# A product of 128 x 256 moved from GpSimd to VectorE in the gated stage of an expert layer

## The chip, the cores and the metric

The kernel runs on one core of one Trainium2 chip. The metric is the device time of one execution in microseconds (us). Engines are written as in the profile: PE is TensorE, DVE is VectorE, ACT is ScalarE, POOL is GpSimd, SP is the queue that issues most DMAs.

## The reference, cut to what matters

The whole kernel computes two transformer blocks on 256 tokens of width 1024. The change lies in the last layer, a mixture of 16384 experts of which each token takes 128 (8 heads of 16), each weighted by a gate:

```python
xb = tokens                                   # (t, 1024)
u = jnp.take(u_tab, eb, axis=0)               # experts' input rows
a = jax.nn.gelu(jnp.einsum('td,thkd->thk', xb, u), approximate=False)
w = (gb * a)                                  # gate x gelu
vv = jnp.take(v_tab, eb, axis=0)
y = jnp.einsum('thk,thkd->td', w, vv)
```

The kernel gathers nothing. It computes gelu(x u) for all 16384 experts, multiplies it by a dense matrix of gates that is zero for the experts not taken, and multiplies the result by the whole value table.

## The kernel before

**The weights' stream.** All weights come as one stream of 512 KB blocks through a ring of four slots. ScalarE copies a block to a rounded form (`w_high`, L496), VectorE subtracts that from the block (`w_low`, L1005, called split below), and TensorE makes each product as three matmuls: high x high, low x high, high x low (L1750 to L1752). A slot is loaded again once it is split.

**The expert layer.** The 16384 experts are 128 blocks of 128. `GE` (in the profile `expert_w`) holds for each block n and each of 256 tokens the product gate x gelu. For the first 66 blocks ScalarE writes the gelu straight into the block's slot. From then on gates are applied while the other blocks are still being computed: this is the gated stage, steps s = 2 to 63, block 64 + s. Slots not yet computed were filled with ones by GpSimd (L458 to L465). In each step

- TensorE computes block 64 + s (`u_block`, 24 matmuls of 256 columns) and then the dense gates of a group of four tokens, group s - 2 (`gates`, eight matmuls, L2311 and L2312), from one-hot tiles.
- ScalarE (`u_tile`) takes the gelu of block 64 + s into one half of a buffer (`GELU`, L921), makes the rounded copy of a later weight block (L496), and scales the one-hots of key 1 by the gates in four instructions (`gate_key1`, L931). `u_tile` waits until the product of block 62 + s has read its half of the buffer.
- GpSimd (`product`, L467 to L474) multiplies the gelu into the block's slot of `GE`.
- VectorE runs, in this order: `weigh` (L1679), which multiplies the gates of one group into four token columns of all 128 slots; `low1` (L1670), the low part of the gates on the one-hots; `hot2` (L1661), the one-hot of key 2 for the next group; a split (L1005); and `hot1` (L1653), the one-hot of key 1, in a single buffer that `gate_key1` and `low1` read.

**What sets the order.** Each engine's order is written out by hand. `weigh` touches all slots and a product touches one slot in all columns, so they must alternate: `product(s)` waits for `weighed` >= s - 2 and the next `weigh` waits for `prod_ok`. In VectorE's loop, step s = 4 i + q, weigh(s - 3) waits for the gates of group s - 3 and for `prod_ok` >= s - 2, which is the product of block 64 + s - 1. The loops on all engines are `Fori(1, 16)`: 15 turns of four steps, s = 4 to 63. Ahead of the loop stand the first product(s), the first weighing and the one-hots of groups 0 to 2; behind it the last groups, interleaved with the first four value blocks, whose weights are split into high and low from `GE` in halves (L968, L1713). Then comes the value stage, 128 blocks of 12 matmuls of 512 columns.

The order of VectorE's loop is this:

```python
with dve.Fori(1, STEPS // 4) as i:
    for q in range(4):
        weigh(q - 3, i * 4, 1)
        low1(q - 2, i * 4)
        hot2(q - 1, i * 4)
        split(b + STEP0 + 3 + q, 1, i * 4)
        hot1(q - 1, i * 4)
```

Of the kernel before, what the change touches and what calls it, by code (L numbers as in the profile page):

```python
# [13 lines left out]
ALU = mybir.AluOpType  # L14
# [42 lines left out]
EXPERT_BLOCKS = 128  # L57
# [5 lines left out]
STEP0 = 64  # L63
FIRST_GATED = STEP0 + 2
STEPS = EXPERT_BLOCKS - STEP0
# [33 lines left out]
def at(static, dyn=None, scale=1):  # L99

    return static if dyn is None else dyn * scale + static


def build(nc, stream, w_dt, cols, small_row, rows, x, mem, keys, out):
# [3 lines left out]
    def sb(name, shape, kb, dt=F32):  # L108
        return nc.alloc_sbuf_tensor_at(name, shape, dt, offset=B0 + int(kb * KB))

    def sem(name):
        return ctx.enter_context(nc.semaphore(name))
# [119 lines left out]
    GELU = sb("gelu_out", [P, 2, SEQ], 75.5)  # L232


    GE = sb("expert_w", [P, EXPERT_BLOCKS, SEQ], 79)
# [105 lines left out]
    tops_ok, gelu_ok, weighed, prod_ok = sem("tops_ok"), sem("gelu_done"), sem("group_weighed"), sem("block_weighed")  # L341
    slots_one, wt_high, wt_low = sem("slots_one"), sem("weighted_high"), sem("weighted_low")
# [36 lines left out]
    def _(pool):  # L379
# [84 lines left out]
        pool.wait_ge(hot_one, 4)  # L464
        pool.memset(GE[:, 80:105, :], 1.0).then_inc(slots_one, 1)  # L465

        def product(s, dyn=None, late=True):  # L467

            pool.wait_ge(gelu_ok, at(STEP0 + s + 1, dyn))
            if late:  # L470
                pool.wait_ge(weighed, at(s - 2, dyn))
            n = STEP0 + s
            slot = GE[:, n, :] if dyn is None else GE[:, bass.ds(dyn + n, 1), :].rearrange("p a t -> p (a t)")
            pool.tensor_tensor(slot, slot, GELU[:, s % 2, :], ALU.mult).then_inc(prod_ok, 1)  # L474

        pool.wait_ge(slots_one, 3)
        product(2, late=False)
        product(3)
        with pool.Fori(1, STEPS // 4) as i:
            for q in range(4):  # L480
                product(q, i * 4)
        pool.dma_start(LAST_GAIN[:], rows[4].partition_broadcast(P)).then_inc(row_in, 16)


# [513 lines left out]
    def _(dve):  # L998
        chain = Chain(dve, dve_chain)

        def split(n0, count, dyn=None):

            for n in range(n0, n0 + count):
                dve.wait_ge(w_high, at(n + 1, dyn))
                dve.tensor_tensor(WL[:, n % SLOTS, :], RING[:, n % SLOTS, :],  # L1005
                                  WH[:, n % SLOTS, :].bitcast(F32), ALU.subtract).then_inc(w_split, 1)
# [355 lines left out]
        for tt in range(TT):  # L1362
            dve.wait_ge(xs_sc, tt + 1)
            s = slice(tt * 4, tt * 4 + 4)
            chain(dve.reduce_max(STAT[:, 24:32][:, s], ACC[:, tt, :].rearrange("p (h m) -> p h m", h=4), AX_X))
            dve.tensor_scalar(STAT[:, 32:40][:, s], STAT[:, 24:32][:, s], -1.0 / 16, None, ALU.mult).then_inc(xs_max, 1)
        for tt in range(TT):
            dve.wait_ge(xs_exp, tt + 1)
            s = slice(tt * 4, tt * 4 + 4)
# [273 lines left out]
        def pairs(row, g, dyn):  # L1643

            t = bass.ds(at(GROUP * g, dyn, GROUP), GROUP)
            return row[:, t].rearrange("p (a b) -> p a b", b=2).unsqueeze(2).to_broadcast([P, GROUP // 2, P, 2])

        def hot1(g, dyn=None):

            if dyn is not None or g >= 1:  # L1650
                dve.wait_ge(key1_ok, at(g, dyn))
                dve.wait_ge(low1_ok, at(g, dyn))
            dve.tensor_tensor(OAE[:], IOTA16[:].unsqueeze(1).to_broadcast([P, GROUP // 2, P, 2]),  # L1653
                              pairs(KEY_T[:, 0, :], g, dyn), ALU.is_equal).then_inc(one1_ok, 1)

        def hot2(g, dyn=None):

            if dyn is not None or g >= 2:
                dve.wait_ge(g_ps, at(g - 1, dyn))
            t = bass.ds(at(GROUP * g, dyn, GROUP), GROUP)  # L1660
            dve.tensor_tensor(OB[:, g % 2, :, :], IOTA[:].unsqueeze(1).to_broadcast([P, GROUP, P]),  # L1661
                              KEY_T[:, 1, t].unsqueeze(2).to_broadcast([P, GROUP, P]),
                              ALU.is_equal).then_inc(key2_ok, 1)

        def low1(g, dyn=None):

            dve.wait_ge(one1_ok, at(g + 1, dyn))
            if dyn is not None or g >= 2:
                dve.wait_ge(g_ps, at(g - 1, dyn))
            dve.tensor_tensor(OAL[:, g % 2, :, :, :], OAE[:], pairs(GATE_LOW, g, dyn), ALU.mult).then_inc(low1_ok, 1)  # L1670

        def weigh(g, dyn=None, blocks=None):

            dve.wait_ge(g_ps, at(g + 1, dyn))
            if blocks:
                dve.wait_ge(prod_ok, at(g + blocks, dyn))
            w = GE[:, :, bass.ds(at(GROUP * g, dyn, GROUP), GROUP)]
            o = 1024 + g % 2 * 512
            dve.scalar_tensor_tensor(w, PS[:, o:o + 512].rearrange("p (t n) -> p n t", n=P), 1.0 / GATE_SCALE, w,  # L1679
                                     ALU.mult, ALU.mult).then_inc(weighed, 1)  # L1680

        split(b + STEP0 + 4, 2)
        dve.wait_ge(rt_ok, 2)
        dve.wait_ge(iota_ok, 2)
# [6 lines left out]
        low1(1)  # L1691
        dve.wait_ge(slots_one, 3)
        dve.wait_ge(gelu_ok, FIRST_GATED)
        dve.wait_ge(prod_ok, 1)
        weigh(0)
        hot2(2)
        hot1(2)
        with dve.Fori(1, STEPS // 4) as i:
            for q in range(4):
                weigh(q - 3, i * 4, 1)  # L1700
                low1(q - 2, i * 4)
                hot2(q - 1, i * 4)
                split(b + STEP0 + 3 + q, 1, i * 4)
                hot1(q - 1, i * 4)
        low1(STEPS - 2)
        split(m + 3, 1)
        hot2(STEPS - 1)
# [722 lines left out]
```

## Time and profile before

| | us |
|---|---|
| median of 3 runs | 1722.03 (1719.54 to 1722.96) |
| profiled execution, its own time | 1721.7 |
| its span in the trace | 1720.0 |
| TensorE busy | 1672.3 (97%) |
| VectorE busy | 1190.6 (69%) |
| ScalarE busy | 934.2 (54%) |
| GpSimd busy | 114.5 (7%) |
| gated stage, from the first product to the last | 1140.86 to 1360.59 |

The 1.7 us between span and time lie around the traced instructions. Shares over the whole span mix stages with different limits: the gated stage takes some 220 us of it. The ends of matmuls are modelled, so the distance between starts says more on TensorE than its busy time. A start in the timeline is when the engine began an instruction; the next one can start before the end shown.

### The profile page before, as it was taken

The numbers are of one execution on the slowest core, as the hardware profiler recorded it, in microseconds if no ns is written. First come the engines' busy times: TensorE is split into PE (matmuls) and PEld (weight loads), VectorE is DVE, ScalarE is ACT, GpSimd is POOL, SyncE is SP. The second block draws the span as 40 slices with busy tenths as digits, with TensorE's granted clock in tenths as the row PEclk, the third lists the DMA queues.
The fourth block names the chain that finished last, engine by engine and source line by source line (L and its number), as shares of the span: only waits on it lengthen the run. The fifth ranks groups of instructions, "written<-read, shape, count | busy, mean of one in ns | idle before, by whom it ended". The sixth has DMA issues, their size and how long they took to land.

```text
span 1720.0 us, 30593 instructions
## 1 busy us (share of the span) xinstructions
PE 1672.3 (97%) x10346; PEld 1482.4 (86%) x10346; DVE 1190.6 (69%) x1827; ACT 934.2 (54%) x1540; POOL 114.5 (7%) x106
## 2 busy tenths in 40 slices
PE   7999999989998999999989999999999999999998
PEld 6888898889897788879979999999999888888887
DVE  5555687487666555466664799989999866666664
ACT  5445546476655544456354444467777654455554
POOL 0000004000000000010010000112222200000000
PEclk9999999989999999999999999999999999999999
DMA  7555453323453555645344455444444365665663
GB/s 260 186 183 183 171 196 123 111 97 124 153 190 123 171 183 184 192 144 187 125 163 158 161 169 195 169 162 146 147 147 148 132 209 193 195 193 190 192 194 122
DMA packets 78814, 286.79 MB, mean 167 GB/s; under 512 B 8864, under 2 KB 9120, under 8 KB 78624
## 3 DMA queue, kind: packets, MB, share of 16 engines
q1 hardware_dynamic: 77888, 282.27, 49.4%
q0 software_dynamic: 864, 3.67, 0.6%
q8 instruction: 41, 0.67, 0.2%
q14 instruction: 21, 0.17, 0.0%
HBM read 284.86 MB, written 1.05 MB: 166 GB/s over the span
## 4 chain that ended last, share of the span: by engine, by line
PE 79%; DVE 10%; issue 6%; ACT 4%; DVEq 1%; DMA 0%; ACTq 0%; POOL 0%; SPq 0%; POOLq 0%
PE ps L1750 24%; PE ps L1752 24%; PE ps L1751 24%; DVE one_at_key L1653 3%; DVE w_low L1005 3%; ACT gate_high_at_key L931 1%; DVE gate_low_at_key L1670 1%; ACT w_high L496 1%; PE ps L1757 1%; PE ps L1839 1%; DVE xT_low L1039 0%; DVE tmp L1090 0%; ACT xn L512 0%; PE ps L2276 0%; DVE h L1092 0%
## 5 line engine op out<-in xcount | busy, mean ns | idle before, releaser
L1005 DVE TENSOR_TENSOR w_low<-ring,w_high 128x1024 fp32r<-128x1024 f32 x532 | 654.2, 1232 | 341.4 <-ACT w_high L496 339.3
L496 ACT ACTIVATE w_high<-ring 128x1024 fp32r<-128x1024 f32 x532 | 559.4, 1056 | 319.2 <-PE ps L1752 312.4
L1750 PE MATMUL ps<-xT_high,w_high 128*128 128x256 f32 x1600 | 462.1, 289 | 1.9 <-DVE xT_low L1039 1.9
L1751 PE MATMUL ps<-xT_high,w_low 128*128 128x256 f32 x1600 | 454.2, 284 | 0.0
L1752 PE MATMUL ps<-xT_low,w_high 128*128 128x256 f32 x1600 | 454.1, 284 | 0.0
L1750 PEld LDWEIGHTS ps<-xT_high,w_high 128*128 128x128 f32 x1600 | 308.2, 193 | 5.9 <-DVE w_low L1005 2.3
L1751 PEld LDWEIGHTS ps<-xT_high,w_low 128*128 128x128 f32 x1600 | 308.4, 193 | 0.7 <-issue 0.5
L1752 PEld LDWEIGHTS ps<-xT_low,w_high 128*128 128x128 f32 x1600 | 308.0, 193 | 0.0
L1750 PE MATMUL ps<-w_high,expert_w_high 128*128 128x512 f32 x512 | 200.5, 392 | 0.4 <-DVE expert_w_low L1713 0.4
L1751 PE MATMUL ps<-w_high,expert_w_low 128*128 128x512 f32 x512 | 200.0, 391 | 0.0
L1752 PE MATMUL ps<-w_low,expert_w_high 128*128 128x512 f32 x512 | 200.0, 391 | 0.0
L1750 PE MATMUL ps<-w_high,xT_high 128*128 128x512 f32 x464 | 187.1, 403 | 11.5 <-DVE xT_low L1039 6.4
L1752 PE MATMUL ps<-w_low,xT_high 128*128 128x512 f32 x464 | 183.4, 395 | 0.0
L1751 PE MATMUL ps<-w_high,xT_low 128*128 128x512 f32 x464 | 183.4, 395 | 0.0
L980 ACT ACTIVATE expert_w_high<-expert_w 128x256 fp32r x124 | 51.8, 418 | 164.9 <-PE ps L1752 164.9
L1750 PEld LDWEIGHTS ps<-w_high,xT_high 128*128 128x128 f32 x464 | 88.7, 191 | 31.5 <-DVE w_low L1005 7.6
L1750 PEld LDWEIGHTS ps<-w_high,expert_w_high 128*128 128x128 f32 x512 | 96.6, 189 | 20.7 <-issue 0.6
L1751 PEld LDWEIGHTS ps<-w_high,expert_w_low 128*128 128x128 f32 x512 | 96.6, 189 | 19.9
L1752 PEld LDWEIGHTS ps<-w_low,expert_w_high 128*128 128x128 f32 x512 | 96.5, 189 | 19.9
L931 ACT ACTIVATE gate_high_at_key<-one_at_key,gate_high 128x128 f16<-128x128 f16 x256 | 82.0, 391 | 52.5 <-DVE one_at_key L1653 52.5
L1731 DVE TENSOR_TENSOR expert_w_low<-expert_w,expert_w_high 128x256 fp32r<-128x256 f32 x124 | 52.7, 425 | 82.3 <-ACT expert_w_high L980 82.3
L1752 PEld LDWEIGHTS ps<-w_low,xT_high 128*128 128x128 f32 x464 | 88.6, 191 | 19.1
(373 smaller groups left out, 2115.1 us busy)
## 6 DMA issues: line engine op xcount, KB each, us to landing
ring<-in_stream SPq DMA_DIRECT2D x532, 512.0 KB, 3.4
row_gain<-in_rows POOLq DMA_DIRECT2D x4, 512.0 KB, 4.4
h<-in_x SPq DMA_DIRECT2D x2, 512.0 KB, 4.3
mem_sb<-in_mem SPq DMA_DIRECT2D x1, 1024.0 KB, 11.3
keys_sb<-in_keys POOLq DMA_DIRECT2D x1, 1024.0 KB, 5.3
out<-result SPq DMA_DIRECT2D x2, 512.0 KB, 2.6
last_gain<-in_rows POOLq DMA_DIRECT2D x1, 512.0 KB, 4.8
cols<-in_cols SPq DMA_DIRECT2D x1, 78.5 KB, 7.4
```

What stands on the lines that cost most here:

```text
L496: act.activation(WH[:, n % SLOTS, :], RING[:, n % SLOTS, :], ACT.Copy).then_inc(w_high, 1)
L931: last = act.activation(OAH[:, g % 2, j, :], OAE[:, j // 2, :, j % 2], ACT.Copy, scale=gate)
L980: act.activation(WTH[:, v % 4, :], slot, ACT.Copy).then_inc(wt_high, 1)
L1005: dve.tensor_tensor(WL[:, n % SLOTS, :], RING[:, n % SLOTS, :], WH[:, n % SLOTS, :].bitcast(F32), ALU.subtract).then_inc(w_split, 1)
L1653: dve.tensor_tensor(OAE[:], IOTA16[:].unsqueeze(1).to_broadcast([P, GROUP // 2, P, 2]), pairs(KEY_T[:, 0, :], g, dyn), ALU.is_equal).then_ ...
L1670: dve.tensor_tensor(OAL[:, g % 2, :, :, :], OAE[:], pairs(GATE_LOW, g, dyn), ALU.mult).then_inc(low1_ok, 1)
L1731: dve.tensor_tensor(WTL[:, v % 4, :], slot, WTH[:, v % 4, :].bitcast(F32), ALU.subtract).then_inc(wt_low, 1)
L1750: pe.matmul(out, high, w_hi, start=start, stop=False, skip_group_check=True)
L1751: pe.matmul(out, low, w_hi, start=False, stop=False, skip_group_check=True)
L1752: return pe.matmul(out, high, w_lo, start=False, stop=stop, skip_group_check=True)
L1757: last = pe.transpose(xt_psum(k, tt)[:, kt, :], XN[:, tt, kt * P:(kt + 1) * P], IDENT[:])
L1839: last = pe.transpose(hidden_psum(p)[:, o:o + P], HN[:, parity, tt, ft * P:(ft + 1) * P], IDENT[:])
```

## The change

GpSimd's product of each of the 62 blocks becomes an instruction of VectorE (`block_weighed`), with the same operands and the same waits. In step s of the loop it handles block 64 + s - 1 and stands first; `low1` moves ahead of `weigh`, so that it lies between the product and the weighing that waits for it. The first product stands ahead of the first weighing and the last one behind the loop. GpSimd keeps one wait for the last gelu, ahead of its load of the last gain. The buffers stay as they are.

```diff
@@ block.gpsimd
-        def product(s, dyn=None, late=True):
-
-            pool.wait_ge(gelu_ok, at(STEP0 + s + 1, dyn))
-            if late:
-                pool.wait_ge(weighed, at(s - 2, dyn))
-            n = STEP0 + s
-            slot = GE[:, n, :] if dyn is None else GE[:, bass.ds(dyn + n, 1), :].rearrange("p a t -> p (a t)")
-            pool.tensor_tensor(slot, slot, GELU[:, s % 2, :], ALU.mult).then_inc(prod_ok, 1)
-
-        pool.wait_ge(slots_one, 3)
-        product(2, late=False)
-        product(3)
-        with pool.Fori(1, STEPS // 4) as i:
-            for q in range(4):
-                product(q, i * 4)
+        pool.wait_ge(gelu_ok, EXPERT_BLOCKS)
         pool.dma_start(LAST_GAIN[:], rows[4].partition_broadcast(P)).then_inc(row_in, 16)
@@ block.vector
+        def block_weighed(s, dyn=None, late=True):
+
+
+            dve.wait_ge(gelu_ok, at(STEP0 + s + 1, dyn))
+            if late:
+                dve.wait_ge(weighed, at(s - 2, dyn))
+            n = STEP0 + s
+            slot = GE[:, n, :] if dyn is None else GE[:, bass.ds(dyn + n, 1), :].rearrange("p a t -> p (a t)")
+            dve.tensor_tensor(slot, slot, GELU[:, s % 2, :], ALU.mult).then_inc(prod_ok, 1)
+
@@
         dve.wait_ge(slots_one, 3)
         dve.wait_ge(gelu_ok, FIRST_GATED)
+        block_weighed(2, late=False)
         dve.wait_ge(prod_ok, 1)
         weigh(0)
         hot2(2)
         hot1(2)
         with dve.Fori(1, STEPS // 4) as i:
             for q in range(4):
+                block_weighed(q - 1, i * 4)
+                low1(q - 2, i * 4)
                 weigh(q - 3, i * 4, 1)
-                low1(q - 2, i * 4)
                 hot2(q - 1, i * 4)
                 split(b + STEP0 + 3 + q, 1, i * 4)
                 hot1(q - 1, i * 4)
+        block_weighed(STEPS - 1)
         low1(STEPS - 2)
         split(m + 3, 1)
         hot2(STEPS - 1)
```

## Rows read from the trace of the kernel before

**Rows 1.** page, part 1: busy time, share of span, instructions

```profile
PE 1672.3 (97%) x10346; PEld 1482.4 (86%) x10346; DVE 1190.6 (69%) x1827; ACT 934.2 (54%) x1540; POOL 114.5 (7%) x106
```

**Rows 2.** busy time by stretch, 13 turns; last columns: clock, DMA share, GB/s

```profile
1159.40:1345.10 185.70, 184.17 (x1666) 174.41 (x1665) 185.70 (x261) 135.87 (x313) 54.74 (x52) 1.00 0.44 147
```

**Rows 3.** timeline of TensorE, one turn; columns: start us, us, engine, line

```profile
1215.96 0.23 PE L2311 MATMUL ps<-gate_high_at_key,one_at_key 128*128 128x128 f16 x1
...
1216.53 0.38 PE L1750 MATMUL ps<-xT_high,w_high 128*128 128x256 f32 x1
...
1219.60 0.23 PE L2311 MATMUL ps<-gate_high_at_key,one_at_key 128*128 128x128 f16 x1
...
1230.82 0.38 PE L1750 MATMUL ps<-xT_high,w_high 128*128 128x256 f32 x1
```

**Rows 4.** timeline of TensorE, way in and first turn

```profile
1147.88 0.28 PE L1752 MATMUL ps<-xT_low,w_high 128*128 128x256 f32 x1
1148.00 0.23 PE L2311 MATMUL ps<-gate_high_at_key,one_at_key 128*128 128x128 f16 x1
...
1148.44 0.37 PE L1750 MATMUL ps<-xT_high,w_high 128*128 128x256 f32 x1
...
1151.39 0.23 PE L2311 MATMUL ps<-gate_high_at_key,one_at_key 128*128 128x128 f16 x1
```

**Rows 5.** timeline of ScalarE beside one steady step; brackets: idle before, releaser

```profile
1218.19 1.28 ACT L931 ACTIVATE gate_high_at_key<-one_at_key,gate_high 128x128 f16<-128x128 f16 x4 [0.80 <-DVE one_at_key L1653]
1219.70 0.38 ACT L921 ACTIVATE gelu_out<-ps 128x256 f32<-128x256 f32 x1 [0.23 <-PE ps L1752]
```

**Rows 6.** timeline of VectorE, one steady step

```profile
1217.09 0.96 DVE L1653 TENSOR_TENSOR one_at_key<-iota,keysT 128x512 f16<-128x512 f16 x1
1217.99 0.69 DVE L1679 SCALAR_TENSOR_TENSOR expert_w<-ps,expert_w 128x512 f32 x1
1218.60 0.41 DVE L1670 TENSOR_TENSOR gate_low_at_key<-one_at_key,gate_low 128x512 f16<-128x512 f16 x1
1218.93 0.69 DVE L1661 TENSOR_TENSOR one_at_key<-iota,keysT 128x512 f16<-128x512 f32 x1
1219.54 1.22 DVE L1005 TENSOR_TENSOR w_low<-ring,w_high 128x1024 fp32r<-128x1024 f32 x1
1220.67 0.97 DVE L1653 TENSOR_TENSOR one_at_key<-iota,keysT 128x512 f16<-128x512 f16 x1
```

**Rows 7.** timeline of VectorE, way in and first turn

```profile
1142.83 0.42 DVE L1653 TENSOR_TENSOR one_at_key<-iota,keysT 128x512 f16<-128x512 f16 x1
1143.17 0.68 DVE L1661 TENSOR_TENSOR one_at_key<-iota,keysT 128x512 f16<-128x512 f32 x1
...
1148.90 0.42 DVE L1653 TENSOR_TENSOR one_at_key<-iota,keysT 128x512 f16<-128x512 f16 x1
```

**Rows 8.** timeline of GpSimd, its products

```profile
1140.86 0.74 POOL L474 TENSOR_TENSOR expert_w<-expert_w,gelu_out 128x256 f32<-128x256 f32 x1 [20.94 <-ACT gelu_out L921]
...
1148.88 1.03 POOL L474 TENSOR_TENSOR expert_w<-expert_w,gelu_out 128x256 f32 x1 [2.90 <-ACT gelu_out L921]
...
1216.69 1.07 POOL L474 TENSOR_TENSOR expert_w<-expert_w,gelu_out 128x256 f32 x1 [2.49 <-ACT gelu_out L921]
1220.35 1.01 POOL L474 TENSOR_TENSOR expert_w<-expert_w,gelu_out 128x256 f32 x1 [2.58 <-ACT gelu_out L921]
```

**Rows 9.** timeline of VectorE, value stage: a 128x256 subtraction

```profile
1375.25 0.42 DVE L1731 TENSOR_TENSOR expert_w_low<-expert_w,expert_w_high 128x256 fp32r<-128x256 f32 x1
1375.59 1.23 DVE L1005 TENSOR_TENSOR w_low<-ring,w_high 128x1024 fp32r<-128x1024 f32 x1
```

**Rows 10.** timeline of TensorE, way out of the gated stage

```profile
1358.80 0.23 PE L2311 MATMUL ps<-gate_high_at_key,one_at_key 128*128 128x128 f16 x1
...
1363.42 0.77 PE L1750 MATMUL ps<-w_high,expert_w_high 128*128 128x512 f32 x1 [0.45 <-DVE expert_w_low L1713]
```

**Rows 11.** busy time by stretch, six microseconds at the way out

```profile
1362.00:1368.00 6.00, 5.21 (x25) 3.99 (x25) 3.85 (x11) 2.36 (x9) 0.00 (x0) 0.72 0.60 228
```

## The prediction

> **What bounds the kernel now.** I read the page first. TensorE is busy for 97% of the span [rows 1], so time comes off only where TensorE waits or is paced by another engine. The next view is the table of busy time by stretch, for the 13 turns of the loop in which all units of the gated stage run evenly. VectorE is busy for all of its 185.70 us [rows 2]. TensorE seems full there too (184.17), but its ends are modelled, so I go by its starts. One turn of four steps takes 14.29 us (1230.82 - 1216.53 in [rows 3]; 185.7 / 13 gives the same), or 3.57 a step. Where nothing held TensorE, in the first turn of the loop, a block's 24 matmuls took 2.95 from their first start to the first gate matmul (1148.44 to 1151.39) and the eight gate matmuls 0.44 (1148.00 to 1148.44) [rows 4]. Closing a turn costs 0.13 to 0.14 more (0.14 taken): 0.57 instead of 0.44 from the gates' first matmul to the next block (1215.96 to 1216.53) [rows 3]. So TensorE alone would need 4 x 3.39 + 0.14 = 13.70 a turn, 0.59 less than it takes. In the steady loop the gates start later than that, just behind ScalarE: its four gate copies end at 1218.19 + 1.28 = 1219.47 [rows 5] and the gates start at 1219.60 [rows 3]. The copies themselves had stood idle 0.80 for VectorE's one-hot [rows 5]. VectorE is the pace maker.
>
> **Where VectorE's 3.57 goes.** One step, start to start [rows 6]: hot1 (L1653) 0.90, weigh 0.61, low1 0.33, hot2 0.61, split 1.13. Sum 3.58. Only hot1 is odd. It takes 0.96 here, but 0.42 with a start-to-start of 0.34 at 1142.83, the same shape [rows 7]. What differs is GpSimd: its product starts at 1216.69, ahead of hot1 at 1217.09, and ends at 1217.76; hot1 ends at 1218.05, 0.29 later [rows 6, 8]. The next one ends at 1221.36 and its hot1 (started 1220.67, 0.97 long) at 1221.64, 0.28 later. So hot1 stands until the product is over and then does its own work. Order matters: at 1148.88 and 1148.90 the two started together, hot1 took its 0.42, and the product stretched to 1.03 against 0.74 for one beside an idle VectorE [rows 7, 8].
>
> **Part by part.** *Removed: 62 products on GpSimd.* Nothing of GpSimd's 0.7 to 1.1 us is on the path as work, but each product holds hot1 for 0.90 - 0.34 = 0.56 of VectorE's time. Gone: -0.56 a step. The POOL queue keeps one wait for the last gelu, as early as before to within the stage's own gain, and behind it the load of the last gain, which is needed only at the end of the kernel: 0. SP's queue gets nothing.
>
> *Added: 62 products on VectorE.* The nearest row is the subtraction over 128x256 float32 from two SBUF tiles, 0.42 long, with the next instruction 0.34 after its start (1375.25 to 1375.59) [rows 9]. I take 0.34; bounds 0.34 and 0.42. VectorE's step becomes 3.58 - 0.56 + 0.34 = 3.36, 13.44 a turn, which is under TensorE's 13.70.
>
> A rule says otherwise. The Trainium skill, VectorE: DVE Perf Modes, section "The DRAIN you can't avoid", holds that a next instruction does not start until the pipe of the one before is empty. By that the product would cost its whole 0.42 and the two short ones around it the same, 3.36 + 3 x 0.08 = 3.60, and nothing would be gained. The trace disagrees: starts 0.34 apart behind instructions of 0.42 [rows 7, 9].
>
> *Waits.* The product waits for ScalarE's gelu, which starts right behind the block's matmuls and lasts 0.38 [rows 5]; behind it in the queue stand low1, weigh, hot2, split and hot1. What TensorE needs of these first is low1, for gates a whole block of matmuls (2.95) later, and hot1, whose copies take 0.13 + 1.28 on ScalarE and are wanted one step after that. Both have slack once VectorE's step is under TensorE's, so the wait costs 0. The product also waits for the weighing two steps back (long done). ScalarE's gelu waits for the product that read the same half of the buffer two blocks before: done over one step earlier, 0. Two waits on VectorE's own results are new: low1 needs hot1's end with only the product between, and weigh needs the product's end with only low1 between. A release costs about 0.23: GpSimd ended at 1217.76 and weigh began at 1217.99 [rows 6, 8]. So 0.42 + 0.23 = 0.65 is due, and cover is 0.34 + 0.34 = 0.68 and 0.34 + 0.33 = 0.67. I take 0 for both; with 0.05 uncovered at each, VectorE needs 3.46, which is 13.84 a turn; fully uncovered is a rival below.
>
> *Moved: low1 ahead of weigh.* Gates get one of their inputs 0.61 - 0.34 = 0.27 earlier; they don't wait for it. 0.
>
> *Way in.* The first product stands alone before the first weighing: 0.65 instead of nothing, but the following hot1, held by GpSimd until now, gives back 0.56. TensorE's first unhindered gates at 1148.00 are not behind by that. 0, bounds 0 and +0.4.
>
> *The loop.* 15 turns x (14.29 - 13.70) = -8.8. Bound by VectorE at 3.46 a step instead: 15 x 0.45 = -6.7.
>
> *Way out.* From the last gates in the loop to the first expert-value matmul TensorE now loses most of 4.62 us (1358.80 to 1363.42) [rows 10]: it waits for hot1 of the last but one group and its copies. Hot1 without GpSimd ends 0.54 sooner, the extra product costs 0.34 behind it, and a VectorE that keeps up reaches hot1 up to 0.9 sooner. Between -0.2 and -1.1; I take -0.6. Right behind that gap the granted clock is 0.72 of full over six microseconds [rows 11], that is 6 x 0.28 = 1.7 us lost at the lower of the two levels (1.2 and 2.4 GHz). A gap about 1 us shorter may or may not keep the clock up. I count 0; bounds 0 and -1.7. The value loop after it is TensorE's own pace: 0.
>
> Sum: -8.8 - 0.6 = -9.4. The profiled execution took 1721.7 us (span 1720.0 and 1.7 around it), 0.3 under the median of 1722.03, so I predict 1712.3.
>
> **Rivals.** *A, VectorE stays the pace maker at 3.42 to 3.52 a step* (uncovered releases, the product at its full 0.42, sequencer work for one more addressed instruction between short ones). For: the cover is 0.02 to 0.03 us thin, and the floors of the two engines are only 0.26 a turn apart. Against: the computed sum is under TensorE's. Time: 15 x (14.29 - 13.9) = -5.9 or so with the way out at -0.2, 1715.6; at 3.52, 1718.3.
>
> *B, TensorE can't go below what it does now.* Now the gates start 3.07 behind their block's first matmul (1216.53 to 1219.60) [rows 3], not 2.95. If that were TensorE's own cost and not ScalarE's lateness, its turn would be 4 x (3.07 + 0.43) + 0.14 = 14.14, a gain of 0.15 x 15 = 2.2 us: 1719.5, no measurable change. Against: in the loop's first turn the gates start 0.12 behind the start of the last block matmul (1147.88 to 1148.00), and the next block reaches its gates in 2.95 [rows 4].
>
> *C, slower: the two waits on its own results stop VectorE.* Place: ahead of low1 and ahead of weigh, each step. If a release needed the predecessor's end plus a fresh issue with nothing overlapped, each costs 0.65 - 0.34 = 0.31: 3.36 + 0.62 = 3.98 a step, 0.41 x 60 = +25 us, 1746. It decides from 3.57 on, that is from 0.21 us uncovered a step. Against: the same kind of wait behind GpSimd was over 0.23 after its end, overlapped with the tail of hot1.
>
> *D, hot1 stays long.* If 0.96 came from its dynamic token address or from the load on SBUF and not from GpSimd, VectorE would need 3.58 + 0.34 = 3.92 and the loop +21 us: 1742. For: the 0.42 rows stand mostly ahead of the loop. Against: the ends 0.28 and 0.29 behind GpSimd's, and the hot1 of 0.42 at 1148.90, which is inside the loop. The Trainium skill has a mechanism for it (SBUF — State Buffer, "Who interferes with whom": a VectorE instruction with two SBUF inputs and a GpSimd one that reads SBUF exclude each other, first come first served), and this trace agrees, 1.03 against 0.42 at 1148.9 included.
>
> **Chances.** Forecast 0.58; A 0.22; B 0.08; C 0.07; D 0.05. About 0.2% (3.4 us) is what a measurement of this kernel can tell from no change. Faster takes the forecast and nearly all of A: 0.79. Same: B and the end of A: 0.09. Slower: C and D: 0.12. The likeliest case alone runs from 1709.5 (way out -1.1 and the clock kept) to 1714. The range adds A up to 3.52 a step, and some half a microsecond on either side for the measurement: 1708.8 to 1718.8. It leaves out B, C and D.
>
> **What the profile after would show.** Right: hot1 at 0.42 throughout; a turn of 13.7 us by TensorE's block starts; gates 0.12 behind the last block matmul; VectorE no longer busy for all of the loop, with short idle times ahead of the product released by gelu. Rival A: VectorE full, a turn of 13.8 to 14.1, gates still behind the copies. B: VectorE idle, TensorE's turn at 14.14. C: gaps between hot1, low1 and weigh released by VectorE itself. D: hot1 at 0.96 with an idle GpSimd. I am wrong if the loop's turn is above 13.9, or if the time won there comes back in the value stage.

## The result

| | before | changed |
|---|---|---|
| median, us | 1722.49 (4 runs, 1719.54 to 1723.50) | 1708.23 (4 runs, 1706.19 to 1709.06) |
| ratio, 95% interval | | 0.992 (0.9905 to 0.9935) |
| profiled execution: own time / span, us | 1721.7 / 1720.0 | 1707.56 / 1705.6 |

The change makes the kernel 14.3 us faster, 0.8%. I had predicted 1712.3 and a range from 1708.8, so the result lies 0.6 us below the range. A second set of six runs of the changed kernel (e11 below) has a median of 1710.10 beside 1721.81 before, 11.7 us less, and that lies inside the range: the miss of the time is no larger than the scatter between sets. The miss of the terms is larger. In the traces below, the stretches that the change touches give -11.0 - 0.9 - 1.5 = -13.4 us, where I had -9.4. The direction and the mechanism were right. Three terms of the sum were too small.

**Where the time went.** The two traces, cut at the same instructions:

| stretch, us | before | changed | difference | forecast |
|---|---|---|---|---|
| start to the block of step 4 | 1145.05 | 1144.06 | -1.0 | 0 |
| from there to the gates behind step 63 | 213.75 | 202.77 | -11.0 | -8.8 |
| from there to the first value matmul | 4.62 | 3.73 | -0.9 | -0.6 |
| first 12 value matmuls | 4.34 | 2.81 | -1.5 | 0 |
| the rest | 352.24 | 352.23 | 0 | 0 |

The sum is -14.4, as the spans say (1720.0 - 1705.6).

The page of the changed kernel, part 1:

```profile
PE 1660.9 (97%) x10346; PEld 1479.3 (87%) x10346; DVE 1179.2 (69%) x1889; ACT 929.7 (55%) x1540; POOL 49.5 (3%) x44
```

VectorE has 62 more instructions than in [rows 1] and is busy for 11.4 us less, although it now does the products too, because the one-hots of the loop no longer stand. Every hot1 is now short (columns: count, then min/median/max in ns, first and last start):

```profile
L1639 DVE TENSOR_TENSOR one_at_key<-iota,keysT x64: 417/421/427, 1137.2 to 1350.5; 128x512 f16<-128x512 f16 x64
```

One step of VectorE, the counterpart of [rows 6] (start us, us, engine, line):

```profile
1214.39 1.22 DVE L991 TENSOR_TENSOR w_low<-ring,w_high 128x1024 fp32r<-128x1024 f32 x1
1215.53 0.42 DVE L1639 TENSOR_TENSOR one_at_key<-iota,keysT 128x512 f16<-128x512 f16 x1
1215.86 0.42 DVE L1676 TENSOR_TENSOR expert_w<-expert_w,gelu_out 128x256 f32 x1
1216.20 0.42 DVE L1656 TENSOR_TENSOR gate_low_at_key<-one_at_key,gate_low 128x512 f16<-128x512 f16 x1
1216.53 0.69 DVE L1665 SCALAR_TENSOR_TENSOR expert_w<-ps,expert_w 128x512 f32 x1
1217.13 0.69 DVE L1647 TENSOR_TENSOR one_at_key<-iota,keysT 128x512 f16<-128x512 f32 x1
1217.73 1.22 DVE L991 TENSOR_TENSOR w_low<-ring,w_high 128x1024 fp32r<-128x1024 f32 x1
1218.87 0.42 DVE L1639 TENSOR_TENSOR one_at_key<-iota,keysT 128x512 f16<-128x512 f16 x1
```

The step is 1218.87 - 1215.53 = 3.34, where it was 3.58. Hot1 frees VectorE 0.33 after its start instead of 0.90, the product costs 0.34, and low1 and weigh start 0.34 and 0.33 behind what stands ahead of them, with no gap. Three steps of a turn are like this one. In the fourth, weigh starts 0.39 to 0.41 behind low1 and the step takes 3.41, so VectorE goes through a turn in 13.43 (products at 1182.32 and 1195.75), where I had forecast 13.44. What holds weigh there for 0.06 is open.

TensorE, at the close of one turn and of the one four steps later, then at the way out (brackets: idle before, releaser):

```profile
1157.17 0.23 PE L2310 MATMUL ps<-gate_high_at_key,one_at_key 128*128 128x128 f16 x1
...
1157.61 0.36 PE L1749 MATMUL ps<-xT_high,w_high 128*128 128x256 f32 x1
...
1171.15 0.36 PE L1749 MATMUL ps<-xT_high,w_high 128*128 128x256 f32 x1
...
1346.83 0.23 PE L2310 MATMUL ps<-gate_high_at_key,one_at_key 128*128 128x128 f16 x1
...
1349.56 0.23 PE L2310 MATMUL ps<-gate_high_at_key,one_at_key 128*128 128x128 f16 x1 [2.11 <-ACT gate_high_at_key L917]
...
1350.56 0.47 PE L1749 MATMUL ps<-w_high,expert_w_high 128*128 128x512 f32 x1 [0.37 <-DVE expert_w_low L1712]
```

A turn is 1171.15 - 1157.61 = 13.54, four steps of 3.385, where it was 14.29 [rows 3]. (The mean of the 15 turns is 13.55, and was 14.28.) Its close costs nothing more: 0.44 from the gates to the next block (1157.17 to 1157.61), not 0.57. The gap at the way out is 1350.56 - 1346.83 = 3.73.

Busy time by stretch, the loop and the six microseconds at the start of the value stage, the counterparts of [rows 2, 11] (PE, PEld, DVE, ACT, POOL busy, granted clock, DMA share, GB/s):

```profile
1157.61:1344.00 186.39, 186.39 (x1765) 184.03 (x1763) 186.22 (x332) 139.16 (x332) 0.00 (x0) 1.00 0.48 156
1350.00:1356.00 6.00, 5.63 (x34) 4.43 (x32) 4.58 (x15) 2.59 (x10) 0.00 (x0) 1.00 0.47 185
```

TensorE is now full. VectorE looks full too (186.22 of 186.39), so this view alone doesn't say which of the two sets the pace; e2 does. The granted clock behind the gap is 1.00 where it was 0.72.

### The profile page after: what moved, and what is told of

The parts are those of the page before. It is cut to its first block, busy times and chain, and to the rows that moved or that the text cites. A ratio compares the mean times of both kernels' runs of the same rounds, so it can differ in the third digit from the quotient of the medians.

```text
span 1705.6 us, 30561 instructions
## 1 busy us (share of the span) xinstructions
PE 1660.9 (97%) x10346; PEld 1479.3 (87%) x10346; DVE 1179.2 (69%) x1889; ACT 929.7 (55%) x1540; POOL 49.5 (3%) x44
## 3 DMA queue, kind: packets, MB, share of 16 engines
HBM read 284.86 MB, written 1.05 MB: 168 GB/s over the span
## 4 chain that ended last, share of the span: by engine, by line
PE 91%; DVE 5%; ACT 3%; issue 1%; DMA 0%; POOL 0%; DVEq 0%; ACTq 0%; POOLq 0%
PE ps L1749 28%; PE ps L1750 28%; PE ps L1751 28%; DVE w_low L991 1%; PE ps L2310 1%; PE ps L2311 1%; PE ps L1756 1%; PE ps L1838 1%; ACT w_high L482 1%; ACT xn L498 1%; DVE xT_low L1025 0%; DVE tmp L1076 0%; PE ps L2275 0%; DVE h L1078 0%; PE ps L2119 0%
## 5 line engine op out<-in xcount | busy, mean ns | idle before, releaser
L1750 PEld LDWEIGHTS ps<-w_high,xT_low 128*128 128x128 f32 x464 | 88.7, 191 | 17.5
```

The costliest lines, as they stand in the source:

```text
L1750: pe.matmul(out, low, w_hi, start=False, stop=False, skip_group_check=True)
```

## The experiments

All are compared with the kernel before on the same chip; 0.2% is about what can be told apart. "Gap" is the distance from the last gates of the loop to the first value matmul.

### e1: the new order without the new place of the product

The kernel before, with `low1` ahead of `weigh`; GpSimd still multiplies.

```diff
-                weigh(q - 3, i * 4, 1)
                 low1(q - 2, i * 4)
+                weigh(q - 3, i * 4, 1)
```

> The kernel before with low1 ahead of weigh, product still on GpSimd. Theory (the gain is hot1 freed from GpSimd, the order only covers a release): no change, ratio 1.000 within 0.001, hot1 still 0.96 us, a turn of four steps 14.29 us. Rival (the order itself gives part of the gain): at least a tenth of the 14 us, ratio 0.999 or less, and a turn under 14.2.

Measured: 1734.97, ratio 1.0076 (1.0056 to 1.0096), so 13.5 us slower than before. The expectation failed. VectorE, one step, and then GpSimd:

```profile
1217.27 0.96 DVE L1653 TENSOR_TENSOR one_at_key<-iota,keysT 128x512 f16<-128x512 f16 x1
1218.36 0.43 DVE L1670 TENSOR_TENSOR gate_low_at_key<-one_at_key,gate_low 128x512 f16<-128x512 f16 x1
...
1216.47 1.49 POOL L474 TENSOR_TENSOR expert_w<-expert_w,gelu_out 128x256 f32 x1 [2.28 <-ACT gelu_out L921]
```

`low1` now stands directly behind the hot1 that it reads and waits for its end: it starts 1.09 after hot1's start, 0.13 after its end (1218.23), where weigh had started 0.90 after it [rows 6]. The turn becomes 15.17. What follows: the order alone costs 13.5 us, and in the change it is harmless only because the product stands in between. What it is good for there, e4 shows.

### e2: the changed kernel without the products

```diff
-                block_weighed(q - 1, i * 4)
                 low1(q - 2, i * 4)
-                weigh(q - 3, i * 4, 1)
+                weigh(q - 3, i * 4)
```

The first and the last product and the waits on `prod_ok` go as well. This kernel leaves the gelu of the last 62 blocks out of the result.

> The changed kernel without the 62 products and the waits on them; the gelu of those blocks is not multiplied in. Theory (after the change TensorE sets the loop's pace and VectorE's added 0.34 us a step is hidden): the loop's turn stays 13.54 us, time 1708 within 1.5 us of the changed kernel. Rival (VectorE still sets it): its step falls to 3.00 us, the turn falls below 13.5 and the time by 2.5 us or more.

Measured: 1708.27, ratio 0.992 (0.9902 to 0.9938), against 1708.23 with the products. The loop by stretch, the columns as above:

```profile
1157.90:1344.00 186.10, 186.10 (x1761) 183.74 (x1759) 174.55 (x276) 137.11 (x331) 0.00 (x0) 1.00 0.47 155
```

VectorE is now idle for 11.6 us of the stretch, and TensorE takes the same step, 2.95 + 0.44. So VectorE's 0.34 a step is wholly hidden, and TensorE is the pace maker of the changed kernel at 3.39 a step. One step of VectorE shows the uncovered release again:

```profile
1214.79 0.42 DVE L1637 TENSOR_TENSOR one_at_key<-iota,keysT 128x512 f16<-128x512 f16 x1
1215.33 0.42 DVE L1654 TENSOR_TENSOR gate_low_at_key<-one_at_key,gate_low 128x512 f16<-128x512 f16 x1
```

Starts 0.54 apart: 0.42 and 0.12.

### e3: two products a step

```diff
+            dve.tensor_tensor(SCRATCH[:], GATE_HIGH[:], GATE_HIGH[:], ALU.mult)
             dve.tensor_tensor(slot, slot, GELU[:, s % 2, :], ALU.mult).then_inc(prod_ok, 1)
```

> The changed kernel with a second 128x256 product on VectorE in every step, into a scratch tile. Theory (VectorE has only 3.385 - 3.34 = 0.045 us a step to spare): its step becomes 3.68, a turn 14.7, the loop 15 x 1.18 = 18 us longer, the way out 1 to 3 more: 1726 to 1730, slower than the kernel before. TensorE's gates come late again, and if the 0.14 us at the close of a turn is the price of late gates, the distance from the first gate matmul to the next block is 0.57 there again; if it was TensorE's own and vanished for another reason, 0.43. Rival (VectorE had slack of some tenths): less than 10 us slower.

Measured: 1728.44, ratio 1.0042 (1.0028 to 1.0057). VectorE's step is 3.68, which is the 3.34 of the changed kernel and 0.34, and the turn 14.71. So VectorE's room below TensorE is 0.05 a step, and whatever is added beyond that is paid in full. TensorE, at the close of a turn:

```profile
1246.56 0.23 PE L2312 MATMUL ps<-gate_high_at_key,one_at_key 128*128 128x128 f16 x1
...
1247.13 0.38 PE L1751 MATMUL ps<-xT_high,w_high 128*128 128x256 f32 x1
```

The 0.57 of [rows 3] is back at all 14 closings that another turn follows, as soon as the gates are late again. (The 15th leads out of the loop, and no block stands behind it.)

### e4: weighing directly behind the product

```diff
                 block_weighed(q - 1, i * 4)
-                low1(q - 2, i * 4)
                 weigh(q - 3, i * 4, 1)
+                low1(q - 2, i * 4)
```

> The changed kernel with weigh directly behind the product and low1 behind it. Theory (a release on VectorE's own result costs 0.42 + 0.23 from the start and only 0.34 passes without cover): 0.31 us more a step, VectorE's step 3.65, a turn 14.6, 16 us in the loop and 1 to 2 at the way out: 1724 to 1727. Rival (the wait overlaps with the next instruction's issue): unchanged, 1708.

Measured: 1727.16, ratio 1.0032 (1.002 to 1.0043). VectorE, product and weighing:

```profile
1215.46 0.41 DVE L1676 TENSOR_TENSOR expert_w<-expert_w,gelu_out 128x256 f32 x1
1216.08 0.69 DVE L1665 SCALAR_TENSOR_TENSOR expert_w<-ps,expert_w 128x512 f32 x1 [0.21 <-DVE expert_w L1676]
```

Start to start 0.62 instead of 0.33: 0.29 a step at one wait. The turn is 14.57 and the loop takes 15.1 more (217.90 against 202.77); the gap (4.58) and the first 12 value matmuls (5.26) add 0.85 and 2.45. This is rival C at one of its two places. It is real, and one short instruction between takes it away.

This kernel is also the bare move: it has the old order, with the product put first. It is 5.7 us slower than the kernel before (1727.16 against 1721.44). So neither half of the change gains alone. The swap costs 13.5 us (e1), the move 5.7, and together they gain 14.3.

### e5: an unrelated product on GpSimd beside the changed kernel

```diff
+        with pool.Fori(1, STEPS // 4) as i:
+            for q in range(4):
+                pool.wait_ge(gelu_ok, at(STEP0 + q + 1, i * 4))
+                pool.tensor_tensor(SCRATCH[:], GATE_HIGH[:], GATE_HIGH[:], ALU.mult).then_inc(scratch_ok, 1)
+                pool.wait_ge(scratch_ok, at(q - 3, i * 4))
         pool.wait_ge(gelu_ok, EXPERT_BLOCKS)
```

Nothing waits for its result, and it touches no tile that VectorE uses there.

> The changed kernel with an unrelated product on GpSimd in every step of the loop, started by the gelu as the old one was: 128x256, both inputs from a tile that nobody writes any more, output to a scratch tile. No engine waits for it. Theory (GpSimd reading SBUF holds a VectorE instruction with two SBUF inputs until it is done): one VectorE instruction behind the split stands 0.5 to 0.6 us, the step becomes 3.9, a turn 15.6, and the time 25 to 36 us above the changed kernel: 1733 to 1744. Rival (hot1 was long for another reason: its own shape, or the wait for the product's data): unchanged, 1708, hot1 0.42.

Measured: 1733.31, ratio 1.0063 (1.0046 to 1.008), 25 us above the changed kernel. GpSimd and hot1:

```profile
1218.33 1.70 POOL L473 TENSOR_TENSOR scratch<-gate_high 128x256 f32<-128x256 f32 x1 [2.06 <-ACT gelu_out L914]
...
1219.49 0.83 DVE L1646 TENSOR_TENSOR one_at_key<-iota,keysT 128x512 f16<-128x512 f16 x1
```

GpSimd ends at 1220.03 and hot1 at 1220.32, 0.29 later, the same distance as in [rows 6, 8] with other tiles. The 1.70 shows the same from GpSimd's side: by the timeline the split before hot1 ran from 1218.35 to 1219.56, and GpSimd's product ended only 0.47 behind it. The step is 3.775, 0.43 above the changed kernel's 3.34, and the turn 15.10. I had expected 15.6, and the time is at the lower end of what I expected. So hot1's stall came from a GpSimd instruction running, not from a tile, a semaphore or hot1's address.

### e6: writes on GpSimd

A product of a single column on GpSimd in each step, and two fills behind it.

```diff
+                pool.tensor_tensor(SCRATCH[:, 0:1], GATE_HIGH[:, 0:1], GATE_HIGH[:, 0:1], ALU.mult).then_inc(scratch_ok, 1)
+                pool.memset(SCRATCH2[:], 0.0).then_inc(scratch_ok, 1)
+                pool.memset(SCRATCH[:, 1:SEQ], 0.0).then_inc(scratch_ok, 1)
```

> The changed kernel with two fills on GpSimd in every step (640 float32 a partition, about 0.6 us together), behind a product of a single column. Theory (only GpSimd's reading is exclusive with VectorE's two-input instructions): hot1 stays at 0.42, the turn at 13.54, the time within 1.5 us of 1708. Rival (any GpSimd access to SBUF holds VectorE): a turn of 15 or more, over 1725.

Measured: 1708.94, ratio 0.9922 (0.9905 to 0.9938); every hot1 takes 0.42 and the turn 13.55. Two steps of GpSimd (POOL) and VectorE:

```profile
1215.76 1.18 POOL L476 TENSOR_TENSOR scratch<-gate_high 128x1 f32<-128x1 f32 x1 [2.57 <-ACT gelu_out L918]
1216.80 0.68 DVE L1676 SCALAR_TENSOR_TENSOR expert_w<-ps,expert_w 128x512 f32 x1
...
1334.28 0.20 POOL L476 TENSOR_TENSOR scratch<-gate_high 128x1 f32<-128x1 f32 x1 [2.29 <-ACT gelu_out L918]
1334.37 0.43 DVE L1687 TENSOR_TENSOR expert_w<-expert_w,gelu_out 128x256 f32 x1
1334.41 0.42 POOL L477 MEMSET scratch<- 128x384 f32 x1
1334.71 0.42 DVE L1667 TENSOR_TENSOR gate_low_at_key<-one_at_key,gate_low 128x512 f16<-128x512 f16 x1
1334.76 0.31 POOL L478 MEMSET scratch<- 128x255 f32 x1
```

The rival is out: fills on GpSimd don't hold VectorE. In the second step they lie beside the product and low1, which have two SBUF inputs and still start 0.34 apart. This is the rule and not the exception. Over the loop the 120 fills take 43.5 us, 36.9 of them beside VectorE instructions with two SBUF inputs, and none of these is longer than in the changed kernel (hot1, product and low1 0.41 to 0.43, hot2 0.68 to 0.69, split 1.21 to 1.23).

The column that GpSimd reads is another matter. It takes between 0.20 and 1.52 us, 0.48 in the median of 61, and over 1 us in four of them. In the first step above it stands beside hot1, the product and low1, which follow each other without a gap, and it ends 0.14 after the weighing has begun, 0.06 after low1's end. So GpSimd's read can wait through three two-input instructions in a row.

### e7: the way out made late again

The changed kernel with two more products on VectorE, once, behind the loop.

```diff
         block_weighed(STEPS - 1)
+        for _ in range(2):
+            chain(dve.tensor_tensor(SCRATCH[:], GATE_HIGH[:], GATE_HIGH[:], ALU.mult))
```

> The changed kernel with two extra 128x256 products with a wait on each, about 1.1 us, on VectorE behind the loop and ahead of low1 of the last group but one; the loop is as it was. TensorE's distance from the last gates of the loop to the first value matmul grows from 3.73 to about 4.8 us. Theory (the length of this gap decides the clock): the granted clock falls to half for 3.4 us behind it as in the kernel before, the first 12 value matmuls take 4.3 instead of 2.81, together +2.6 us, 1711. Rival (the clock fell in the kernel before because of the looser loop ahead of the gap): it stays at full, +1.1.

Measured: 1710.39 (two runs), ratio 0.9928 (0.9908 to 0.9947); span 1707.8, 2.2 above the changed kernel. TensorE's first value matmul, and then the stretch from 1350 to 1356:

```profile
1351.21 0.47 PE L1752 MATMUL ps<-w_high,expert_w_high 128*128 128x512 f32 x1 [1.10 <-DVE expert_w_low L1715]
```

```profile
1350.00:1356.00 6.00, 4.89 (x21) 3.73 (x20) 3.65 (x11) 1.68 (x6) 0.00 (x0) 0.72 0.51 172
```

The gap is 4.47, 0.74 longer, and the granted clock over these six microseconds is 0.72 again, as in [rows 11], where the changed kernel has 1.00. The first 12 value matmuls take 4.41 instead of 2.81. So a wait of 0.74 cost 0.74 + 1.6. I had expected a gap of 4.8; the rest came as expected. So the -1.5 of the first table came of the shorter gap: behind it the clock stayed at its upper level (2.4 GHz), and with the longer one it fell.

### e8: a better way out

The gap at the way out is the largest stop left. In it, by the changed kernel's timeline of ScalarE, come the last gelu, a rounded copy of 1.05 and only then the key-1 copies that TensorE waits for:

```profile
1347.02 0.38 ACT L907 ACTIVATE gelu_out<-ps 128x256 f32<-128x256 f32 x1 [0.89 <-PE ps L1751]
1347.30 1.05 ACT L482 ACTIVATE w_high<-ring 128x1024 fp32r<-128x1024 f32 x1
1348.24 1.26 ACT L917 ACTIVATE gate_high_at_key<-one_at_key,gate_high 128x128 f16<-128x128 f16 x4
```

The edit puts the first two value halves ahead of the last two groups' gates on all three engines. ScalarE's last turn is written out, and its copy and key-1 work stand behind the first halves:

```diff
@@ ScalarE
+        act.activation(GELU[:, 1, :], PS[:, 512:512 + SEQ], ACT.Gelu).then_inc(gelu_ok, 1)
         act.wait_ge(weighed, GROUPS // 2)
         high_half(0, 0)
         high_half(1, 0)
+        gate_key1(STEPS - 2)
+        split(m + 3, 1)
         high_half(2, 0)
         high_half(3, 0)
+        gate_key1(STEPS - 1)
@@ VectorE
-        low1(STEPS - 2)
-        split(m + 3, 1)
-        hot2(STEPS - 1)
...
         low_half(1, 0)
+        low1(STEPS - 2)
+        hot2(STEPS - 1)
...
+        split(m + 3, 1)
         weigh(STEPS - 2)
@@ TensorE
-        gates(STEPS - 2)
...
             if v == 1:
+                gates(STEPS - 2)
                 gates(STEPS - 1)
```

> The changed kernel with another way out of the gated stage: the last gelu and the first two half tiles of high parts ahead of the last copies on ScalarE, their low parts right behind the last product on VectorE, and on TensorE the first two value half blocks ahead of the gates of the last two groups. Theory (in the gap of 3.73 us TensorE waits only for the order of the others' work): the gap shrinks to about 1.5 us, no full idle stretch over 1.2, and the time falls by 1.5 to 2.2 us to about 1706.3. Rival (the gates of the last groups or the split of the fourth value block come late in turn): less than 1 us gained, the waits appear behind the first value half blocks.

Measured: 1705.24, ratio 0.99 (0.9883 to 0.9916), an interval that overlaps the changed kernel's, so what was won is read from the traces. The first value matmul now comes 1.53 behind the loop's last gates (1345.15):

```profile
1346.68 0.47 PE L1757 MATMUL ps<-w_high,expert_w_high 128*128 128x512 f32 x1 [0.90 <-DVE expert_w_low L1717]
```

From the loop's last gates to the third value half block it takes 5.26 instead of 6.97, so 1.7 is won there, as expected. The span is 3.4 shorter; the other 1.7 lies far ahead, where a spell of low clock near 254 us lasted 3.4 us here and 6.8 in the changed kernel's profile.

### e9: longer turns

The kernel of e3 with TensorE's loop in turns of eight steps, one run.

```diff
-        with pe.Fori(1, STEPS // 4) as i:
-            for q in range(4):
-                u_block(STEP0 + q, i * 4)
-                gates(q - 2, i * 4)
+        with pe.Fori(0, 7) as i:
+            for q in range(4, 12):
+                u_block(STEP0 + q, i * 8)
+                gates(q - 2, i * 8)
```

> The kernel with two products on VectorE a step (TensorE's gates late in every step), with TensorE's loop in turns of eight steps instead of four; the other engines' loops as they were. Theory (0.14 us is what closing TensorE's own turn costs when its gates are late): the distance from the first gate matmul to the next block is 0.57 at every eighth step only, 0.43 in between, where it was 0.57 at every fourth; VectorE sets the pace at 14.7 a turn of four, so the time stays at 1728 within 2. Rival (the 0.57 comes from another engine's turn of four steps): still at every fourth step.

Measured: 1730.81, 0.8 above what I had expected. Against the profile of e3 the loop takes the same (219.9); the time ahead of step 4 is 1.85 longer and the first 12 value matmuls 0.84. The distance from the gates to the next block is 0.57 to 0.62 at the six closings (every eighth step) that another turn follows, and 0.43 or 0.44 everywhere else. It is 0.43 also at the seventh, behind step 59, where the loop ends, though the gates were late there too. A closing:

```profile
1174.89 0.23 PE L2312 MATMUL ps<-gate_high_at_key,one_at_key 128*128 128x128 f16 x1
...
1175.46 0.38 PE L1751 MATMUL ps<-xT_high,w_high 128*128 128x256 f32 x1
```

So the 0.14 belongs to TensorE's own turn, to going back to its start. With e3 and the changed kernel beside it: there it is paid only where the gates at the close had to wait. Why (the queue may not get past the branch while it waits) is only argued. One closing of all the profiles doesn't fit: in e8 the first one, behind step 7, takes 0.51 with gates on time.

### e10 and e11: both ends, and the changed kernel again

e10 is e8 with one split moved behind the one-hots on the way in. e11 is the changed kernel, unaltered, in the same set of runs.

```diff
-        split(b + STEP0 + 6, 1)
         hot1(1)
         hot2(1)
         low1(1)
+        split(b + STEP0 + 6, 1)
```

> The kernel with the other way out, and on the way in VectorE's split of weight block 70 of the expert layer's first product moved behind the one-hots of group 1. Theory (TensorE stands 1.11 us ahead of the gates of group 1, since hot1 of that group waits behind this split and the split waits for ScalarE): that stand goes, 1.1 us less than with the other way out alone, ratio to the kernel before 0.989. Rival (ScalarE's copies for group 1 still come behind its gelu and its high part and are late): less than 0.3 us.

> The changed kernel itself, beside the other two: 1708.2 within 1.5 us, a turn of 13.54, the way out 3.73; ahead of the gated stage it may differ from the first profile by one or two spells of low clock of 3.4 us.

Measured: e10 1707.02, ratio 0.9906 (0.9892 to 0.9921); e11 1710.10, ratio 0.9926 (0.9915 to 0.9938). e11 is 0.4 above the band that I had given; its turn and its way out are as expected. TensorE ahead of step 4's block, in e11 and then in e10:

```profile
1146.10 0.23 PE L2310 MATMUL ps<-gate_high_at_key,one_at_key 128*128 128x128 f16 x1 [0.94 <-ACT gate_high_at_key L917]
```

```profile
1145.04 0.23 PE L2318 MATMUL ps<-gate_high_at_key,one_at_key 128*128 128x128 f16 x1
...
1145.48 0.36 PE L1757 MATMUL ps<-xT_high,w_high 128*128 128x256 f32 x1
```

The stand is gone: step 3 takes 3.39 instead of 4.49. Both profiles have the same low-clock spells ahead (10.2 us near 252 and 10.2 near 368), so they compare cleanly: 1705.2 against 1708.1 of span, -2.9, of which 1.1 is the way in and 1.8 the way out. The medians differ by 3.1, though the intervals of the two ratios touch. By the traces e10 is about 3 us faster than the changed kernel, and by the medians 15 faster than the kernel before. Against e8 its ratio can't be told apart (0.9906 and 0.99); what it has over e8 is the 1.1 us that the trace shows at the way in.

## Why the prediction was right, and where it fell short

**Right.** Hot1's stall was GpSimd's doing and is gone with it: 0.42 at all 64, and e5 brings a like one back with an unrelated product. The product costs VectorE 0.34, start to start, and not its whole 0.42. I had set a rule of the Trainium skill (VectorE: DVE Perf Modes, "The DRAIN you can't avoid") against this. I had read it too narrowly: the same paragraph goes on that a next op that is not held starts earlier. With that the trace agrees: in the step above every instruction starts 0.33 or 0.34 behind a short one of 0.42. The pace passes to TensorE (e2: without the products nothing changes). Both covers hold: in three steps of four product, low1 and weigh follow each other without a gap, and in the fourth weigh is 0.06 late. The products' removal and the way in cost nothing: the stand of 0.94 ahead of step 4 is in both traces. The 1.0 us in the first line of the table is not put down to the change: a low-clock spell near 367 us lasted 10.2 us in the profile of before and 6.8 in the other (3.4 us at half the clock are 1.7 of work; but for that the two stretches agree within 0.7), and the length of this spell differs between kernels that are the same there (10.2 in e1, e2, e4, e6; 6.8 in e3, e5, e7). The changed kernel itself reached the block of step 4 at 1144.06 in its first profile and at 1146.54 in its second (e11).

**Step 1 that failed: "Closing a turn costs 0.13 to 0.14 more ... So TensorE alone would need 4 x 3.39 + 0.14 = 13.70 a turn".** I read the 0.14 from a stage in which the gates were late in every step, and took it for TensorE's own floor. The runs show 13.55: the 0.14 is paid only while the gates wait (e3, e9). The 15 turns took 14.28 each and then 13.55, so the loop gained 15 x 0.73 = 11.0, where I had 8.8, and nearly all of the 2.2 between them is the 0.14 at each close. The trace of before showed it. Ahead of the gated stage TensorE runs the same blocks in turns of four with nothing late, and from 960 to 1134 us no two of its 1450 matmuls start more than 0.121 apart, closings included. I had taken 2.95 and 0.44 from the first turn because nothing held TensorE there, but the 0.14 from a held one.

**Step 2 that failed: the clock at the way out, "I count 0; bounds 0 and -1.7".** It was -1.5. The bound was right and the value taken was the wrong end. In the profiles with a gap of 3.73 (this kernel, e2, e6, e11) or 1.53 (e8, e10) the clock stayed up; in those with 4.47 (e7), 4.58 (e4), 4.62 (before), 4.81 (e1), 5.04 (e5) and 5.29 (e3, e9) it fell. My reason for 0 was only that a shorter gap "may or may not" keep it. The lower end of my range did allow for this term, but for no floor of TensorE under 13.70; that is why the result lies outside. A slip in adding made the range reach lower than my terms do. With the way out at -1.1 and the clock kept, my terms give 1721.7 - 8.8 - 1.1 - 1.7 = 1710.1, not 1709.5, so by them the range should have begun some 0.6 us higher. (And 1721.7 is the profiled execution's time; from the median of 1722.03 the forecast is 1712.6.)

**A size: the way out itself**, -0.9 where I took -0.6, within my bounds of -0.2 and -1.1.

**A size: the release.** I took 0.23 for both waits, from a release by another engine. That was only an upper bound: weigh began at 1217.99, 0.06 before hot1's end, so it may have waited for hot1 and not for the release. VectorE's own is 0.12 to 0.13 behind hot1 (e1, e2) and 0.21 behind the product (e4). The cover is thus thinner at the weighing (0.67 for 0.63) than at low1 (0.68 for 0.55). It changed nothing in the sum; the step came out at 3.34, 0.02 under mine.

**One sign that I had set up read otherwise.** I wrote that VectorE would no longer be busy for all of the loop. It is, to 0.2 us. VectorE came into the loop behind: at 1162.12 its product began 0.99 us after the gelu that it needs. With 13.43 a turn against TensorE's 13.55 it made good 0.12 a turn, and only from 1266 on does one product a turn wait, for 0.12, of which 0.03 shows as idle time, since its instructions otherwise start some 0.08 before the end of the one ahead. So VectorE has 0.12 a turn to spare as it runs here, and 0.2 by e3, where the 0.06 at weigh is gone; I had 0.26. Who sets the pace had to be asked by e2.

**The rivals.** A (VectorE at 3.42 to 3.52) is out by the step of 3.34. B (TensorE's turn at 14.14) is out by 13.54: the gates start 0.12 behind the last block matmul (1157.05 and 1157.17). C is out as a whole, but e4 and e1 show its place and its price: 0.29 and 0.19 a step where the cover is missing. D (hot1 long by itself) is out by the 0.42 and by e5. For the exclusion itself the Trainium skill (SBUF — State Buffer, "Who interferes with whom") has the rule that I had cited, and e5 and e6 agree with it from both sides: 0.83 for hot1 behind GpSimd, 1.18 for one column on GpSimd behind VectorE. It also says that a GpSimd instruction that only writes SBUF doesn't contend, and the fills of e6 agree.

**What stays open.** Why a late wait makes the close of a turn dearer, what holds weigh for 0.06 in every fourth step, and what sets off the low-clock spells far ahead of the change, which move single profiles of one kernel by some 1.7 us for each 3.4 us of low clock.

## What to carry to other kernels

A small instruction on an otherwise idle engine is not free if it holds a neighbour: look for one operation that takes longer in a stretch than the same shape elsewhere, and see what ends just before it does. When a wait on an engine's own result can't be avoided, put one independent instruction between; here that was worth 0.29 us a step. Take the floor of the next bottleneck from a stretch in which that engine is never late, all of its terms, since costs that lateness itself brings vanish with it.

## What the runs showed that I had not expected

- Closing a turn of TensorE's loop costs 0.14 us when the matmuls ahead of it were released late, and nothing when they were on time (0.57 against 0.44, in all profiles but for one closing of e8).
- Swapping two instructions of VectorE, with no work added, cost 13.5 us (e1), since a reader then stood directly behind its writer. Moving the product without the swap cost 5.7 (e4). Only the two together gain.
- A one-column product on GpSimd took 0.20 to 1.52 us, by what VectorE ran beside it, while fills on GpSimd cost VectorE nothing (e6).
- A stop of 0.74 us more at the way out cost 2.3 us, the granted clock falling from 1.00 to 0.72 over six microseconds behind it (e7).
